# Prompt attention of a transformer block on one core: tiles unrolled, probabilities turned by transposes, the three branches scaled apart by factor rows that go through DRAM

## Chip, cores and metric

The kernel runs on one core of one Trainium2 chip. The metric is the device time of one execution in microseconds, the median of several runs.

## The reference

One layer of a decoder block on a prompt of 1024 tokens and on 8 sampled requests of 4 tokens: feed-forward, mixer, feed-forward, norm. Only the prompt's attention inside the mixer matters here. There are 8 query heads of width 64, in 2 groups that share keys and values. Each head has three branches: compressed attention over 64 block summaries, selected attention (with 1024 tokens and at most 16 blocks of 64 every causal key is selected) and a window of 512. Each branch has its own softmax and a gate for each token and head:

```python
s = jnp.einsum('btgrd,bngd->bgrtn', qg, kc).astype(jnp.float32) * ATTN_SCALE
p = masked_softmax(s, blk_end[None, :] <= q_pos[:, None])
...
o = gates[..., 0:1] * o_c + gates[..., 1:2] * o_s + gates[..., 2:3] * o_w
return jnp.concatenate([o.reshape(B, T, NSA_WIDTH), pool_out], axis=-1) @ w_out
```

## The kernel before, in words

The program is a sequence of stages with a barrier between them: compress the cache of the samples, feed-forward, input projection, pooling, compress the prompt, prompt attention (`stage_attend_prompt`, L1580), sample attention, output projection, feed-forward, finish. Each stage writes one program for each engine, and the engines meet by semaphores only; every engine works off its own list in order.

**Tiles.** The prompt attention has an outer loop (`Fori`) of two passes, one for each key head `g`, and in it eight tiles `qt` of 128 queries. Each tile has four steps `r`, one for each query head of the group. In a step the kernel makes the scores of head `r` of tile `qt` and at the same time a quarter of the value products of tile `qt-1`. After tile 7 a ninth round holds only value work (the drain), and the next pass then starts anew.

**Scores.** Keys and queries are doubled (POOL, `duplicate`, L1679), transposed on PE in turns of four (L1890) and split into a high and a low part by ScalarE (`high`, L1719) and VectorE (`low`, L1785). A pass begins with the `LEAD`, four turns for the keys and one for the first query tile. `selected_scores` (L1898) and `window_scores` (L1914, window and compressed keys together) write PSUM; VectorE takes the negated maxima (L1853, L1857, L1859), ScalarE the exponentials with their sums (L1757, L1763, L1765). They fill one PSUM tile each, so the next head's scores wait for the exponentials.

**Values.** A value unit is one block of up to 128 keys of one branch: tile `qt` has qt+1 selected units, min(qt+1, 5) window units and one compressed unit, 3, 5, 7, 9, 11, 12, 13 and 14 for tiles 0 to 7, 74 in a pass. In a unit PE multiplies the probabilities of the four heads by diagonal matrices (L1884), which transposes and scales them at once; ScalarE copies the high part (L1733), VectorE subtracts for the low part (L1798), and PE adds two products to one output bank (L1948, L1949). Turns alternate between two banks, so a turn waits for the subtraction of the turn two before. The product of a unit is issued behind the turn of the next. The order of turns is written out by `turns` and `steps` (L1618, L1622).

**Factors.** The diagonals hold gate divided by sum. VectorE makes the factors for two heads at a time after steps 2 and 3 (`factors`, L1802: three or four small operations), POOL multiplies them with an identity (L1700), and the first turn of the next tile waits for both (L1881).

**Output.** All three branches add up in one output bank, since they are already scaled. The upper half holds the product with the low part of the values; ScalarE copies it (L1738) and VectorE adds the halves for each head into `mixT` (L1830), one tile later.

SP has nothing to do in this stage. Queues of DMAs are idle in it but for instruction fetches.

```python
for h in range(GROUP):
    tr = pe.matmul(bank[0:rows, h * P:(h + 1) * P], probs[qt % 2][:, h, lo:lo + rows],
                   diag[:, qt % 2, h, branch, :], start=True, stop=True)
```

## Time and profile before

| | us |
|---|---|
| median of three runs | 3279.51 |
| lowest, highest | 3276.8, 3280.99 |
| the profiled execution | 3281.28 |
| its span | 3279.6 |
| PE busy | 2924.5 (89%) |
| VectorE busy | 1448.3 (44%) |
| ScalarE busy | 905.5 (28%) |
| POOL busy | 311.1 (9%) |

The stage of the change runs from about 1621 to 2099 us of the span. In the tables of windows and of groups PE is the multiplying part of TensorE and PEld its weight loads, DVE is VectorE, ACT ScalarE. A busy time is the time in which an instruction of the engine was under way; PEclk is the granted clock of TensorE as a share of 2.4 GHz, so 0.50 is 1.2 GHz. "idle before" of a group is the time its engine stood still directly before one of its instructions, with what ended it.

### The profile page before, as it was taken

What the parts mean: (1) busy time and instruction counts of PE and PEld (TensorE: products, weight loads), DVE (VectorE), ACT (ScalarE), POOL (GpSimd) and SP (SyncE); (2) the same over time, 40 slices, a digit from 0 to 9 for tenths busy, and PEclk for the clock granted to TensorE, in tenths of its full rate; (3) what the DMA queues carried; (4) which work ended last, traced back from release to release, by engine and by line L of the source; (5) the groups of instructions that cost most, each with busy time, mean ns of one, the idle gap of its engine ahead of it and who ended that gap; (6) DMA issues with size and microseconds to landing.
All of it is one profiled execution on the core that took longest, in us unless ns stands there. A gap on an engine that the chain in (4) does not pass through costs nothing. (4 is left out here: it accounts for less than half of the span.)

```text
span 3279.6 us, 48743 instructions
## 1 busy us (share of the span) xinstructions
PE 2924.5 (89%) x18374; PEld 2688.3 (82%) x18374; DVE 1448.3 (44%) x2808; ACT 905.5 (28%) x1537; POOL 311.1 (9%) x294
## 2 busy tenths in 40 slices
PE   4999989999999997885789789687799999999997
PEld 4889879999999996884667667433589999999996
DVE  4444455544444445013255456312326454444445
ACT  4665651111111102111245345233222111111112
POOL 3444410000000001000011011211000000000000
PEclk9999999999999998997579879888899999999999
DMA  4212133211111102102100000365322111111101
GB/s 158 110 56 110 62 105 105 64 38 38 40 50 42 47 0 87 33 26 77 35 1 1 2 1 1 125 183 158 112 58 62 42 53 49 38 38 51 38 13 53
DMA packets 168574, 193.84 MB, mean 59 GB/s; under 512 B 11431, under 2 KB 154536, under 8 KB 165679
## 3 DMA queue, kind: packets, MB, share of 16 engines
q1 hardware_dynamic: 161623, 141.58, 14.2%
q0 software_dynamic: 6816, 50.49, 4.2%
q8 instruction: 81, 1.33, 0.2%
q14 instruction: 54, 0.44, 0.0%
HBM read 178.30 MB, written 17.91 MB: 60 GB/s over the span
## 5 line engine op out<-in xcount | busy, mean ns | idle before, releaser
L407 ACT ACTIVATE f_act_gate<-f_act_gate 128x352 f32<-128x352 f32 x132 | 65.8, 498 | 1186.2 <-DVE f_act_gate L464 1186.1
L501 DVE SCALAR_TENSOR_TENSOR trunk<-f_down,trunk 128x352 f32<-128x352 f32 x528 | 275.8, 524 | 207.8 <-PE f_down L104 207.8
L102 PE MATMUL f_up<-f_h_hi,f_gu_hi 128*128 128x352 f32 x1056 | 344.6, 326 | 0.0
L102 PE MATMUL f_gate<-f_h_hi,f_gu_hi 128*128 128x352 f32 x1056 | 344.3, 326 | 0.0
L104 PE MATMUL f_up<-f_h_hi,f_gu_lo 128*128 128x352 f32 x1056 | 342.8, 325 | 0.0
L104 PE MATMUL f_gate<-f_h_hi,f_gu_lo 128*128 128x352 f32 x1056 | 342.5, 324 | 0.0
L102 PE MATMUL f_down<-f_a_hi,f_wd_hi 128*128 128x352 f32 x1056 | 340.6, 323 | 0.0
L103 PE MATMUL f_gate<-f_h_lo,f_gu_hi 128*128 128x352 f32 x1056 | 340.5, 322 | 0.0
L103 PE MATMUL f_up<-f_h_lo,f_gu_hi 128*128 128x352 f32 x1056 | 340.1, 322 | 0.0
L103 PE MATMUL f_down<-f_a_lo,f_wd_hi 128*128 128x352 f32 x1056 | 338.5, 321 | 0.0
L104 PE MATMUL f_down<-f_a_hi,f_wd_lo 128*128 128x352 f32 x1056 | 338.1, 320 | 0.0
L102 PE MATMUL cs_sum<-cs_x_hi,cs_w_hi 128*128 128x256 f32 (+1 forms) x768 | 229.9, 299 | 32.6 <-DVE cs_x_lo L1152 21.4
L104 PE MATMUL cs_sum<-cs_x_hi,cs_w_lo 128*128 128x256 f32 (+1 forms) x768 | 217.5, 283 | 0.0
L103 PE MATMUL cs_sum<-cs_x_lo,cs_w_hi 128*128 128x256 f32 (+1 forms) x768 | 217.4, 283 | 0.0
L102 PEld LDWEIGHTS f_gate<-f_h_hi,f_gu_hi 128*128 128x128 f32 x1056 | 199.6, 189 | 1.3 <-DVE f_gu_lo L447 1.1
L102 PEld LDWEIGHTS f_up<-f_h_hi,f_gu_hi 128*128 128x128 f32 x1056 | 199.9, 189 | 0.0
L1884 PE MATMUL at_turn_bank<-at_diag,at_probs 128*128 128x128 f32 (+1 forms) x1184 | 177.7, 298 | 24.6 <-POOL at_diag L1700 20.3
L1884 PEld LDWEIGHTS at_turn_bank<-at_diag,at_probs 128*128 128x128 f32 (+1 forms) x1184 | 162.4, 203 | 45.3 <-issue 39.6
L103 PEld LDWEIGHTS f_gate<-f_h_lo,f_gu_hi 128*128 128x128 f32 x1056 | 198.8, 188 | 0.2
L103 PEld LDWEIGHTS f_up<-f_h_lo,f_gu_hi 128*128 128x128 f32 x1056 | 198.9, 188 | 0.0
L103 PEld LDWEIGHTS f_down<-f_a_lo,f_wd_hi 128*128 128x128 f32 x1056 | 198.4, 188 | 0.0
L102 PEld LDWEIGHTS f_down<-f_a_hi,f_wd_hi 128*128 128x128 f32 x1056 | 198.1, 188 | 0.0
(333 smaller groups left out, 5812.3 us busy)
## 6 DMA issues: line engine op xcount, KB each, us to landing
as_pages<-in_cache_kv_slc_dram SPq DMA_DIRECT2D x192, 128.0 KB, 2.3
f_gu_raw<-in_w_ffn_gate_dram SPq DMA_DIRECT2D x44, 512.0 KB, 4.5
f_gu_raw<-in_w_ffn_up_dram SPq DMA_DIRECT2D x44, 512.0 KB, 5.7
f_wd_raw<-in_w_ffn_down_dram SPq DMA_DIRECT2D x22, 1024.0 KB, 5.0
as_pages<-in_cache_kv_slc_dram POOLq DMA_DIRECT2D x64, 128.0 KB, 3.2
in_w_raw<-in_w_in_dram SPq DMA_DIRECT2D x4, 1304.0 KB, 5.9
x_saved<-trunk SPq DMA_DIRECT2D x1, 4224.0 KB, 16.2
trunk<-x_saved SPq DMA_DIRECT2D x1, 4224.0 KB
```

The source lines that it names most:

```text
L102: pe.matmul(out, w_hi, x_hi, start=first, stop=False)
L103: pe.matmul(out, w_hi, x_lo, start=False, stop=False)
L104: return pe.matmul(out, w_lo, x_hi, start=False, stop=last)
L407: act.activation(act_gate[:, b, :], act_gate[:, b, :], ACT.Silu).then_inc(silu_done, 1)
L501: dve.scalar_tensor_tensor(xT[:, m, chunk(c)], down_bank[n % 4][:, 0:CH], 0.5, xT[:, m, chunk(c)], ALU.mult, ALU.add).then_inc(down_free, 1)
L1884: tr = pe.matmul(bank[0:rows, h * P:(h + 1) * P], probs[qt % 2][:, h, lo:lo + rows], diag[:, qt % 2, h, branch, :], start=True, stop=True)
```

## The change

The loop over two key heads becomes a straight list of 16 tiles `n`, with `g, qt = divmod(n, QT)`. The drain of tile 7 and the lead of tile 8 are interleaved, and only tile 15 has a drain by itself. All waits are on constants, and the no-ops before PE's groups are gone. In a step PE now issues the first turn, the window scores, the other turns, and then the selected scores of the next head.

Value turns are plain transposes of the exponentials. Each branch of a tile has an output bank of its own (two banks in turn). The factors of a tile, 12 columns in all (3 branches by 4 heads), are computed once by VectorE in the first step of the next tile, transposed on PE into 12 rows (a turn "f", first in step 1), copied by ScalarE, written to DRAM by SP (6 KB) and, when that has landed, read back by SP into all 128 partitions (`spread`, 768 KB). VectorE multiplies each branch's bank by its part of `spread` (`scale`), behind the first turn of the following branch; POOL adds the three branches and the two halves (`gather`). The key and value splits of the second head are made branch by branch, as the values of the first become free.

The core of the diff:

```diff
+            @block.sync
+            def _(sp):
+                for n in range(TILES):
+                    sp.wait_ge(hi_done, at[("f", n)] + 1)
+                    sp.dma_start(saved_rows[n % 2], factor_rows[:]).then_inc(rows_saved, 16)
+                    sp.wait_ge(rows_saved, 16 * (n + 1))
+                    if n:
+                        sp.wait_ge(scaled_done, 3 * n)
+                    sp.dma_start(spread[:].rearrange("p b r n -> p (b r) n"),
+                                 saved_rows[n % 2].unsqueeze(0).to_broadcast([P, ROWS, P])).then_inc(spread_landed, 16)
...
+                def gather(n):
+                    g, qt = divmod(n, QT)
+                    pool.wait_ge(scaled_done, 3 * n + 2)
+                    pool.tensor_tensor(scaled[:, 0], scaled[:, 0], scaled[:, 1], ALU.add).then_inc(added, 1)
+                    pool.wait_ge(scaled_done, 3 * n + 3)
+                    pool.wait_ge(added, 4 * n + 1)
+                    pool.tensor_tensor(scaled[:, 0], scaled[:, 0], scaled[:, 2], ALU.add).then_inc(added, 1)
+                    pool.wait_ge(added, 4 * n + 2)
+                    pool.tensor_copy(upper[:], scaled[HD:2 * HD, 0]).then_inc(added, 1)
+                    pool.wait_ge(added, 4 * n + 3)
+                    for half, sem in enumerate((added, out_taken)):
+                        pool.tensor_tensor(mixT[half * HD:(half + 1) * HD, 2 * g:2 * g + 2, qt * P:(qt + 1) * P],
+                                           scaled[0:HD, 0, half::2, :], upper[:, half::2, :], ALU.add).then_inc(sem, 1)
...
+    def lead(n):
+        own = [("k", n, b, half) for b in range(2) for half in range(2)] + [("q", n)]
+        values = quarter(n - 1, 0) if n else []
+        mixed = [x for pair in zip(own, values) for x in pair]
+        return mixed + own[len(values):]
+
+    def turns(n, r):
+        own = [("q", n + 1)] if r == 2 and n + 1 < TILES and not leads(n + 1) else []
+        if n == 0:
+            return own
+        values = [] if r == 0 and leads(n) else quarter(n - 1, r)
+        return ([("f", n - 1)] if r == 1 else []) + values + own
...
+                def scale(n, b):
+                    dve.wait_ge(pv_done, products[("v", n, ends[n][b])] + 1)
+                    dve.wait_ge(spread_landed, 16 * (n + 1))
+                    if n:
+                        dve.wait_ge(out_taken, n)
+                    dve.tensor_tensor(scaled[:, b], out_bank[(3 * n + b) % 2][:].rearrange("p (r n) -> p r n", r=GROUP),
+                                      spread[:, BRANCHES[b]], ALU.mult).then_inc(scaled_done, 1)
...
                     if x[0] == "v":
-                        _, qt, u = x
-                        branch, lo, rows, _ = value_units(qt)[u]
-                        if u == 0:
-                            pe.wait_ge(diag_ready, 2 * QT * g + 2 * (qt + 1) + ONE)
-                        pe.nop(nofuse=True)
+                        _, n, u = x
+                        branch, lo, rows, _ = value_units(n)[u]
+                        pe.wait_ge(exped[0 if branch == SLC else 1], GROUP * (n + 1))
                         for h in range(GROUP):
-                            tr = pe.matmul(bank[0:rows, h * P:(h + 1) * P], probs[qt % 2][:, h, lo:lo + rows],
-                                           diag[:, qt % 2, h, branch, :], start=True, stop=True)
+                            tr = pe.transpose(bank[0:rows, h * P:(h + 1) * P], probs[n % 2][:, h, lo:lo + rows],
+                                              K["ident"][:])
...
                     else:
-                        pe.wait_ge(dup_ready, DUPS * g + dups[x] + 1)
-                        pe.nop(nofuse=True)
-                        for i in range(4):
-                            tr = pe.transpose(bank[:, i * P:(i + 1) * P],
-                                              dup[dups[x] % 2][:, i].rearrange("p c d -> p (c d)"), K["ident"][:])
+                        pe.wait_ge(factor_ready, x[1] + 1)
+                        tr = pe.transpose(bank[0:ROWS, 0:P], factor[:, x[1] % 2].rearrange("p b r -> p (b r)"),
+                                          K["ident"][:])
...
+                for n in range(TILES + 1):
+                    for r in range(GROUP):
+                        xs = turns(n, r)
+                        first = lead(n) if r == 0 and leads(n) else xs[:1]
+                        rest = xs if r == 0 and leads(n) else xs[len(first):]
+                        for x in first:
+                            through(x)
+                        if r == 0 and leads(n):
+                            selected_scores(n, r)
+                        if n < TILES:
+                            window_scores(n, r)
+                        for x in rest:
+                            through(x)
+                        following = (n, r + 1) if r + 1 < GROUP else (n + 1, 0)
+                        if following[0] < TILES and not (following[1] == 0 and leads(following[0])):
+                            selected_scores(*following)
+                value_product()
...
+    saved_rows = nc.dram_tensor("saved_rows", [2, 12, P], F32).ap()
```

`through` issues a turn and then the product of the unit before it. VectorE's list follows PE's: the selected maximum, `low` of the first turn, the window maxima, the factors of the tile before (in step 0), `low` of the others with `scale` behind the unit that follows a branch's last one.

## Rows read from the trace of the kernel before

**Rows 1.** The page: its first line, PE's busy time, the granted clock in 40 slices.
```profile
span 3279.6 us, 48743 instructions
...
PE 2924.5 (89%) x18374; PEld 2688.3 (82%) x18374; DVE 1448.3 (44%) x2808; ACT 905.5 (28%) x1537; POOL 311.1 (9%) x294
...
PEclk9999999999999998997579879888899999999999
```

**Rows 2.** Windows of the stage: us, busy per engine, PEclk, DMA share, GB/s.
```profile
1621.00:1707.00 86.00, 66.59 (x333) 52.54 (x333) 42.98 (x112) 39.53 (x126) 15.56 (x16) 0.70 0.00 1
1707.00:1825.00 118.00, 106.88 (x679) 87.24 (x679) 69.98 (x135) 60.86 (x148) 13.41 (x11) 0.96 0.00 1
1825.00:1857.00 32.00, 26.03 (x147) 21.11 (x145) 11.91 (x22) 9.68 (x17) 2.63 (x3) 0.89 0.00 1
1857.00:1872.00 15.00, 4.89 (x20) 3.79 (x20) 4.60 (x9) 5.54 (x9) 2.45 (x4) 0.61 0.02 6
...
2067.00:2099.00 32.00, 23.73 (x142) 19.81 (x142) 12.87 (x26) 9.55 (x16) 1.47 (x1) 0.95 0.00 1
sum 478.00, PE 398.98 PEld 321.53 DVE 250.00 ACT 220.94 POOL 60.87; mean PE 57.00 PEld 45.93 DVE 35.72 ACT 31.56 POOL 8.70
```

**Rows 3.** Groups of instructions of the stage: busy, mean ns, idle before and its releaser.
```profile
L1884 PE MATMUL at_turn_bank<-at_diag,at_probs 128*128 128x128 f32 (+1 forms) x1184 | 177.7, 298 | 24.6 <-POOL at_diag L1700 20.3 <-PE at_out_bank L1949 2.1 <-DVE at_turned_lo L1798 1.0
...
L1798 DVE TENSOR_TENSOR at_turned_lo<-at_turn_bank,at_turned_hi 128x512 fp32r<-128x512 f32 (+1 forms) x148 | 102.1, 690 | 154.2 <-ACT at_turned_hi L1733 154.1
...
L1700 POOL TENSOR_TENSOR at_diag<-ident,at_factor 128x768 f32<-128x768 f32 x32 | 47.0, 1469 | 346.5 <-DVE at_factor L1821 346.5
...
L1830 DVE TENSOR_TENSOR trunk<-at_out_bank,at_upper 64x128 f32 x64 | 18.1, 283 | 15.0 <-ACT at_upper L1738 14.1
...
L1738 ACT ACTIVATE at_upper<-at_out_bank 64x512 f32<-64x512 f32 x16 | 9.5, 594 | 3.7 <-PEq L1953 3.4
...
L1815 DVE RECIPROCAL at_factor<-at_factor 128x6 f32<-128x6 f32 x32 | 6.1, 191 | 1.1
```

**Rows 4.** Timeline of PE in tile 6: start, length, instruction.
```profile
1780.63 0.64 PE L1890 MATMUL at_turn_bank<-ident,at_dup 128*128 128x128 f32 x4
1781.10 1.06 PE L1884 MATMUL at_turn_bank<-at_diag,at_probs 128*128 128x128 f32 x8
1781.91 0.47 PE L1948 MATMUL at_out_bank<-at_turned_hi,at_v_split 128*128 128x512 f32 x1
```

**Rows 5.** Timeline of PE: the first selected scores of tiles 1 and 4.
```profile
1643.76 0.33 PE L1910 MATMUL at_slc_bank<-diagonal,ident 128*128 128x128 bf16 x1
...
1706.69 0.23 PE L1910 MATMUL at_slc_bank<-diagonal,ident 128*128 128x128 bf16 x1
```

**Rows 6.** Timeline of PE: products in the drain of the first pass.
```profile
1849.59 0.47 PE L1948 MATMUL at_out_bank<-at_turned_hi,at_v_split 128*128 128x512 f32 x1 [0.22 <-DVE at_turned_lo L1798]
...
1852.76 0.47 PE L1948 MATMUL at_out_bank<-at_turned_hi,at_v_split 128*128 128x512 f32 x1 [0.22 <-DVE at_turned_lo L1798]
```

**Rows 7.** DMA issues: KB each, us from issue to landing.
```profile
op_w_raw<-in_w_out_dram SPq DMA_DIRECT2D x8, 512.0 KB, 4.1
...
f_wd_raw<-in_w_ffn_down_dram SPq DMA_DIRECT2D x22, 1024.0 KB, 5.0
...
cp_raw<-out_dram SPq DMA_DIRECT2D x1, 1024.0 KB, 13.7
...
cs_pe<-in_pe_cmp_k_dram SPq DMA_DIRECT2D x1, 8.0 KB, 1.7
...
gates_saved<-z SPq DMA_DIRECT2D x1, 3.0 KB, 4.0
```

**Rows 8.** Windows of the true transposes of L1236 and L2299 alone: busy, PEclk, DMA.
```profile
100.00:120.00 20.00, 4.22 (x28) 3.27 (x28) 1.00 0.62 224
...
2240.00:2260.00 20.00, 5.69 (x28) 4.39 (x28) 0.68 0.25 78
```

More of the change, by code:

```diff
@@ L1629, in stage_attend_prompt, with quarter @@
[L1629 to L1637 removed]
+    def quarter(n, r):
+        count = len(value_units(n))
+        return [("v", n, u) for u in range(count * r // GROUP, count * (r + 1) // GROUP)]
@@ new lines, in stage_attend_prompt @@
+    order = [x for n in range(TILES + 1) for r in range(GROUP)
+             for x in (lead(n) if r == 0 and leads(n) else []) + turns(n, r)]
+    at = {x: i for i, x in enumerate(order)}
+    dups = {x: i for i, x in enumerate([x for x in order if x[0] in "kq"])}
+    dup_order = list(dups)
+    values_order = [x for x in order if x[0] == "v"]
+    products = {x: i for i, x in enumerate(values_order)}
+    ends = [[max(u for u, unit in enumerate(value_units(n)) if unit[0] == branch) for branch in BRANCHES]
+            for n in range(TILES)]
@@ L1639, in stage_attend_prompt @@
+    behind = {}
+    for x, follower in zip(values_order, values_order[1:]):
+        if x[2] in ends[x[1]]:
+            behind[follower] = (x[1], ends[x[1]].index(x[2]))
     with ExitStack() as scope:
@@ L1950, in value_product @@
+                    pe.matmul(bank[:], values, turned_lo[v % RING][0:rows, :], start=False,
                               stop=last).then_inc(pv_done, 1)
[L1951 to L1973 removed]
@@ new lines, in through @@
+                def through(x):
+                    turn(x)
+                    value_product()
+                    if x[0] == "v":
+                        pending.append(x)
+                for n in range(TILES + 1):
+                    for r in range(GROUP):
+                        xs = turns(n, r)
+                        first = lead(n) if r == 0 and leads(n) else xs[:1]
+                        rest = xs if r == 0 and leads(n) else xs[len(first):]
+                        for x in first:
+                            through(x)
+                        if r == 0 and leads(n):
+                            selected_scores(n, r)
+                        if n < TILES:
+                            window_scores(n, r)
+                        for x in rest:
+                            through(x)
+                        following = (n, r + 1) if r + 1 < GROUP else (n + 1, 0)
+                        if following[0] < TILES and not (following[1] == 0 and leads(following[0])):
+                            selected_scores(*following)
```

465 lines of the change are left out of this document (226 added, 239 removed).

## The prediction, made before the changed kernel was run

> **What bounds the kernel now.** First the page: over the whole span PE is busy 89% of the time, and the granted clock is full in most slices but dips in those of the prompt attention, 19 to 25 [rows 1]. The change touches that stage alone, so the second view is the table of windows over it, from 1621 to 2099 us, 478 us of the span. Its seven stretches are two passes of one loop body over the two key heads: tiles 0 to 3 (86 us, PE busy 77%, mean clock 0.70), tiles 4 to 7 (118 us, PE busy 91%, clock 0.96), the drain of the last tile's 14 value units (32 us), and 15 us between the passes in which PE is busy 4.9 us [rows 2]. So three different limits: latency and a slow clock in the small tiles, PE in the large ones, and plain idleness at the seam. VectorE is busy 70 of the 118 us of the large tiles and ScalarE 61, so neither is far behind PE.
>
> Third, the groups of instructions with what they waited for [rows 3]. The 592 multiplications by a diagonal (L1884) are the stage's largest PE group: 1184 instructions, two for each product, while the true transposes of the doubled keys and queries are one each [rows 4]. PE stands idle 20.3 us before them waiting for the diagonals that POOL makes.
>
> Fourth, the timeline of PE at full clock in tile 6 [rows 4]. Four true transposes start at 1780.63 and what follows starts at 1781.10: 0.47 us. One turn through diagonals starts at 1781.10 and its successor at 1781.91: 0.81 us. A turn that is a true transpose is 0.34 us shorter.
>
> **The change, part by part** (negative is saved; all in us).
>
> a) *Turns become transposes.* 148 value turns, 0.34 each, 50 of PE time. What reaches the end depends on the limit. In the large tiles, where PE is the bound, there are 9+11+12+13 = 45 value units per pass, 90 in all: at most 90 x 0.34 = 31. In the drain, where the two-bank loop turn, copy, subtract, product binds, the products two units apart start at 1849.59 and 1852.76 [rows 6]: 3.17 for two, and shortening one turn per loop leaves 2.83, so 0.17 a unit. I take 0.27 for the 90: **-24** (0 to -31). The small tiles are latency bound: nothing.
>
> b) *No diagonals.* PE's 20.3 of waiting on POOL [rows 3] has no successor: the transposed operand is the exponentials, done before the tile ends. POOL's 47.0 of diagonals leaves with it. **-18** (-12 to -20).
>
> c) *The seam.* From 1825, when the first pass has its last scores, to 1872, when the second pass starts its first [rows 2], pass 47 us. In the new order the 14 value units of tile 7 lie between the five lead turns and the scores of tile 8. The same work on PE: 14 units at about 1.4 (1.59 less 0.17) is 20, the lead turns another 5, since their copies and subtractions alternate with those of values. 47 - 25 = **-22** (-10 to -32, the latter if tile 8's scores also run under the values).
>
> d) *The last drain and its end.* 14 x 0.17 = 2.4 saved; but after the last product come one scaling, then on POOL two adds of 128x512, a copy of 64x512 and two half adds. POOL's 128x768 multiply takes 1.47 [rows 3], so about 1.0 per full add and 0.6 for each of the rest: 4.5 in all with the scaling, against 0.59 + 4 x 0.28 = 1.7 for the copy and four adds now; the earlier branches are added while PE still works. **0** (-2 to +3).
>
> e) *VectorE.* Added: 48 scalings of 128x512 out of PSUM; the nearest row is the subtraction of the same shape, 0.690 [rows 3], so 33. Removed: 64 adds at 0.283, 18, and half of the factor operations, three of about 0.17 to 0.19 for 16 pairs, 8 [rows 3]. Net +7 on an engine that is busy 250 of the 478 us [rows 2]. **+4** (0 to +7). ScalarE loses 16 copies and gains 16 smaller ones: nothing. POOL trades 47 for about 16 x 4.3 = 69; it is busy 13% now, and its result is asked for more than a step later.
>
> f) *The turned factor rows.* 16 times a transpose on PE at 0.12, with a wait of PE for the factors, which VectorE now makes in the tile's next step; behind that wait stand the window scores. **+5** (+2 to +15).
>
> g) *The round trip through DRAM.* SP issues a 6 KB write and, when it has landed, a read of 768 KB into 128 partitions. No row shows a re-read of one place. The write: an 8 KB load lands in 1.7, a 3 KB store into DRAM in 4.0 [rows 7]; I take 2. The read: between 4.1 for 512 KB and 5.0 for 1024 KB of weights, 4.6; the highest row is 13.7, for 1024 KB read back from an output. With about 0.8 of issue and waits the trip is 7.4. The Trainium skill (DMA: Bandwidth & Descriptors, section on the anatomy of one DMA) gives 2.0 us and 436 GB/s, an estimate of 3.8 for the read; no run here shows it for a repeated source, and the sum would be some 10 lower by it. VectorE needs the rows at the first scaling, one step and about 1 us after the factor turn. A step in tiles 1 to 3 is (1706.69-1643.76)/12 = 5.2 now [rows 5], say 4.5 after; in tiles 4 to 7 (118/16) 7.4, say 6.5. So VectorE stands still about 2 in each of the four smallest tiles of a pass and hardly in the others, and behind it on its queue stand the window maxima, hence the exponentials, hence PE. 8 x 2 = **+16** (0 to +80).
>
> h) *Scores one step ahead.* The selected scores of the next head are issued before the step ends, and waits are on constants without extra no-ops. PE's waits for exponentials in the two kinds of scores and for issue are short and many. **-12** (0 to -20).
>
> i) *The clock.* Stretches with idle PE lose the full clock: 0.61 at the seam, 0.70 in the small tiles [rows 2]. A faster PE is idle more often in the large tiles; it may fall there at times, as at 1825 to 1857 (0.89). **+8** (0 to +40). A drain window at 0.95 and the large tiles at 0.96 speak against more. Stretches elsewhere with true transposes in the stream show both: full in one where they take 4.2 of 20 us, 0.68 in one where they take 5.7 [rows 8]. The Trainium skill (TensorE: Matmul & The Clock Gate, part 4, on transposes) says that the full clock doesn't engage for transposes; the first of these rows disagrees for a mixed stream, the second leaves room for it. That is a rival below.
>
> Sum: -24-18-22+0+4+5+16-12+8 = **-43**. The profiled execution took 3281.28 around a span of 3279.6; the median of the runs is 3279.51, so the sum is set against that: 3279.5 - 43 = **3237**.
>
> **The rivals.**
> 1. *The repeated read is slow, and VectorE waits for it in every tile: slower.* With R the whole trip and 6.5 the mean distance to the first scaling, the stall is 16 x (R - 6.5), against 59 saved by everything else. It decides at R = 10.2, a read of about 7.4. A read at 9.2, midway between 4.6 and 13.7, gives R = 12.0, +88 - 59 = +29: 3309. For: 6 KB read 128 times has no counterpart here. Against: the weight rows, and no other traffic in the stage (DMA share 0.00 in the windows). Chance 0.13.
> 2. *The clock falls in the large tiles.* PE's work there at full clock is 107 less 15 for the shorter turns, 92 per pass. With the clock at its lower level for half of the time that takes 92/0.75 = 123 instead of the 108 forecast, +30 for both passes: 3267; for the whole time 184, +152. The Trainium skill's sentence above points this way. For: the drop to 0.68 in rows 8. Against: PE gets busier as it slows, and the products and scores remain. Chance 0.12, a quarter of it slower than now.
> 3. *PE's saved time isn't used*: the chain turn, copy, subtract, product or VectorE binds in the large tiles too, and a) and h) are worth nothing: 3279.5 - 43 + 36 = 3272.5. For: VectorE and ScalarE at 60% and 52% there. Against: PE at 91%. Chance 0.12.
> 4. *PE's work sets the pace almost everywhere*, the trip is hidden and the seam disappears: -31-20-32-20+7 = -96 and with f) and i) 3195. Chance 0.13.
>
> Forecast case 0.50, from 3210 to 3262.
>
> **How the numbers follow.** The likeliest case gives 3237. The range has to take in rivals 2 to 4 and the foot of rival 1: 3190 to 3295, which leaves out about 0.2. About 0.2%, 6.6 us, is what a measurement of this kernel can tell from no change. Slower by more: rival 1 and a quarter of rival 2, 0.16. The same: a quarter of rival 2 and half of rival 3, 0.09. Faster: the rest, 0.75.
>
> **What would show it.** Right: one instruction for each turned head instead of two and 0.47 for a turn at full clock; no wait on POOL before turns; no stretch without scores or products at the middle of the stage; large tiles at about 27 us instead of 29.5; the spread landing about 4.6 after its issue; a VectorE wait for a DMA of 1 to 3 in small tiles only. Wrong: a spread that lands after more than 7 us, VectorE idle before scalings in all tiles, a granted clock under 0.85 in the large tiles, or a PE that is idle there on the subtractions by as much as its turns became shorter.

## The result and the profile of the changed kernel

The changed kernel takes **3173.5 us** (median of 4 runs, 3171.8 to 3174.5) beside 3280.3 for the kernel before (3276.8 to 3282.8). The ratio is 0.9675, with a 95% interval of 0.9658 to 0.9692: 107 us are saved where 43 were forecast, and the time lies below the range. The first lines of the page that answer to [rows 1], the changed kernel:

```profile
span 3172.3 us, 46324 instructions
...
PE 2825.5 (89%) x17798; PEld 2592.6 (82%) x17798; DVE 1457.5 (46%) x2742; ACT 904.5 (29%) x1536; POOL 338.6 (11%) x342
...
PEclk9999999999999999899559989789899999999999
```

PE does 99 us less and is still busy 89% of the span. The clock dips below 9 tenths in slices 19, 20, 23 and 25 (counted from 0), among others; the stage begins at 1620, in slice 20, so the 5 of slice 19 lies ahead of it, as most of slice 19 does before [rows 1]. Nearly all of the difference in time, 105 us, lies in the stage: it now lasts 373 us, from 1620, in place of 478. Its windows answer to [rows 2]; columns as there:

```profile
1620.00:1691.40 71.40, 56.09 (x275) 43.27 (x275) 43.06 (x99) 39.08 (x124) 14.88 (x20) 0.69 0.09 34
1691.40:1795.70 104.30, 87.22 (x551) 66.01 (x549) 80.33 (x131) 67.76 (x160) 26.20 (x31) 1.00 0.09 31
1795.70:1818.00 22.30, 19.53 (x107) 15.64 (x106) 12.24 (x28) 11.44 (x37) 2.22 (x4) 0.77 0.11 36
1818.00:1872.40 54.40, 44.64 (x218) 32.52 (x217) 36.00 (x78) 30.08 (x95) 15.97 (x18) 0.75 0.13 44
1872.40:1959.30 86.90, 74.74 (x475) 56.96 (x474) 68.84 (x114) 58.50 (x142) 19.69 (x22) 1.00 0.10 38
1959.30:1993.00 33.70, 20.96 (x122) 15.06 (x121) 18.62 (x29) 13.04 (x25) 9.16 (x10) 0.93 0.07 24
sum 373.00, PE 303.18 PEld 229.46 DVE 259.10 ACT 219.89 POOL 88.13; mean PE 50.53 PEld 38.24 DVE 43.18 ACT 36.65 POOL 14.69
```

The stretches are tiles 0 to 3 (71.4 us), tiles 4 to 7 (104.3), the seam up to tile 9 (22.3), tiles 9 to 11 (54.4), tiles 12 to 15 (86.9) and what follows the last selected scores (33.7). In the large tiles the clock is now 1.00, where it was 0.96 [rows 2]; the small tiles stand at 0.69 and 0.75, where tiles 0 to 3 stood at 0.70. The groups of instructions of the stage, changed kernel, answer to [rows 3]:

```profile
L1936 PE MATMUL at_turn_bank<-ident,at_probs 128*128 128x128 f32 (+1 forms) x592 | 97.4, 295 | 0.0
...
L2007 PE MATMUL at_out_bank<-at_turned_hi,at_v_split 128*128 128x512 f32 x132 | 68.3, 517 | 33.8 <-DVE at_turned_lo L1826 33.8
...
L1838 DVE TENSOR_TENSOR at_scaled<-at_out_bank,at_spread 128x512 f32<-128x512 f32 x48 | 32.6, 680 | 4.3 <-DMA at_spread<-saved_rows 4.0 <-PE at_out_bank L2008 0.2
...
L1869 DVE TENSOR_SCALAR at_factor<-at_sums 128x12 f32<-128x12 f32 x16 | 8.2, 512 | 0.1
...
L1878 DVE TENSOR_TENSOR at_factor<-at_factor,z 128x12 f32<-128x12 f32 x16 | 6.2, 386 | 0.6
...
L1945 PE MATMUL at_turn_bank<-ident,at_factor 128*12 128x128 f32 x16 | 4.9, 309 | 11.3 <-DVE at_factor L1878 11.3
```

L1936 is now one instruction a head: 97.4 us in place of 177.7 [rows 3]. No wait on POOL stands before it. PE's largest wait is for the subtractions (33.8), and VectorE waits 4.0 us for the spread in the whole stage. The factor turn (L1945), though, is waited for 11.3 us, and the two factor operations ahead of it take 512 and 386 ns on average. Before, on half as many columns, they took 162 and 166:

```profile
L1821 DVE TENSOR_TENSOR at_factor<-at_factor,z 128x6 f32<-128x6 f32 x32 | 5.3, 166 | 4.7 <-DVE at_factor L1818 0.5
L1813 DVE TENSOR_SCALAR at_factor<-at_sums 128x6 f32<-128x6 f32 x32 | 5.2, 162 | 4.5 <-ACT at_probs L1765 2.7 <-issue 1.8
```

Where the 107 went, by the length of the tiles (from the first diagonal block of selected scores of a tile to that of a later one, the points of [rows 5]):

| Stretch (us) | before | loop written out (experiment 1) | and transposes (4) | and no diagonals (4) | changed |
|---|---|---|---|---|---|
| tiles 1 to 3 | 62.9 | 62.0 | 55.0 | 49.7 | 50.9 |
| tiles 4 to 6 | 87.6 | 84.9 | 77.3 | 74.2 | 68.0 |
| start of tile 7 to start of tile 9 | 90.0 | 78.8 | 71.0 | 66.5 | 58.6 |
| tiles 9 to 11 | 64.5 | 61.4 | 55.1 | 49.8 | 54.4 |
| tiles 12 to 14 | 87.5 | 86.2 | 78.7 | 74.2 | 68.0 |

The three middle columns are experiments, told next; each column is one execution. Every stretch gives something: the two of small tiles 12.0 and 10.1 us, the two of large tiles 19.6 and 19.5, the seam 31.4. The transposes gave 7.0 and 6.3 in the small tiles, where the prediction had nothing. What came after the diagonals, from the fourth column to the last, gave 7.9 at the seam and 6.2 in each stretch of large tiles, but took 1.2 and 4.6 in the small ones.

### The profile page after: what moved, and what is told of

The parts are those of the page before. It is cut to its first block and busy times, and to the rows that moved or that the text cites. A ratio compares the mean times of both kernels' runs of the same rounds, so it can differ in the third digit from the quotient of the medians.

```text
span 3172.3 us, 46324 instructions
## 1 busy us (share of the span) xinstructions
PE 2825.5 (89%) x17798; PEld 2592.6 (82%) x17798; DVE 1457.5 (46%) x2742; ACT 904.5 (29%) x1536; POOL 338.6 (11%) x342
## 5 line engine op out<-in xcount | busy, mean ns | idle before, releaser
L102 PE MATMUL cs_sum<-cs_x_hi,cs_w_hi 128*128 128x256 f32 (+1 forms) x768 | 229.4, 299 | 33.8 <-DVE cs_x_lo L1152 22.6
L104 PEld LDWEIGHTS f_up<-f_h_hi,f_gu_lo 128*128 128x128 f32 x1056 | 198.0, 188 | 0.0
L104 PEld LDWEIGHTS f_gate<-f_h_hi,f_gu_lo 128*128 128x128 f32 x1056 | 198.0, 187 | 0.0
```

What stands on the lines that cost most here:

```text
L102: pe.matmul(out, w_hi, x_hi, start=first, stop=False)
L104: return pe.matmul(out, w_lo, x_hi, start=False, stop=last)
```

## The experiments

Times are medians; "saved" is against the kernel before as it ran beside them (medians of 3278.8 to 3282.8). Differences from the changed kernel are between sets of runs, and its interval of 0.0017 on either side of the ratio is 5.6 us: under that, one needs the trace. A trace is one execution, though. In four kernels whose large tiles have the same work in the same order (the changed one and those of experiments 8 and 9) tiles 4 to 6 take 68.0, 68.0, 68.0 and 68.9 us; tiles 1 to 3 take 50.9, 51.0, 47.6 and 48.0, at a granted clock of 0.77, 0.77, 0.86 and 0.86. So the large tiles can be compared to some tenths, but 3 us in a stretch of small tiles can be the clock alone.

**1. The loop alone.** The kernel before, its loop over the two key heads written out on four engines.

```diff
-                with pe.Fori(0, N_KV) as g:
+                for g in range(N_KV):
```

> The kernel before with its loop over the two key heads written out, so that every wait is on a constant and no register is worked out; order, diagonals, no-ops and the drain before the second lead stay. Theory 1 (the gain of 107 us comes from the merged seam, the shorter turns and the new order): only the jump at the seam (PE idle from 1856 to 1864 us) and a little at each wait go, 5 to 15 us faster than before, 3265 to 3275. Theory 2 (registers in front of each wait had slowed every handover between engines, and constants are most of the gain): 40 us or more faster, 3240 or less.

Measured: 3258.1, 0.9932 (0.9915 to 0.9948), 24 saved, between the two forecasts. This is the seam without any interleaving. Timeline of PE at the seam, the first lead turn of the second pass with the idle time before it, first in the kernel before, then in this one (start, length, instruction):

```profile
1864.02 1.86 PE L1890 MATMUL at_turn_bank<-ident,at_dup 128*128 128x128 f32 x8 [7.28 <-issue]
```

```profile
1849.01 1.06 PE L1890 MATMUL at_turn_bank<-ident,at_dup 128*128 128x128 f32 x8 [0.30 <-PE at_out_bank L1949]
```

Before, PE stood still 7.28 us between the last product of the first pass and the first lead turn, on issue: nothing in the records releases it but the loop's end. What takes the time there is not shown. Written out, the gap is 0.30. From tile 7 to tile 9 the loop is worth 11.2 us (table); the rest of the gain is spread over the tiles in pieces of 1 to 3 us, and some of it may be the clock.

**2. The transposes alone.** The kernel before, the loop kept and the diagonals still made and waited for. It leaves out the scaling by gate over sum.

```diff
-  tr = pe.matmul(bank[...], probs[...], diag[...], start=True, stop=True)
+  tr = pe.transpose(bank[...], probs[...], K["ident"][:])
```

> The kernel before with true transposes of the probabilities in place of the products with diagonals. The diagonals are still made and waited for, and leave the output: the value products are not scaled by gate over sum. Everything else stays. Theory 1: the shorter turns alone are worth 25 to 40 us in the old order (90 units of the large tiles at 0.3 to 0.46, little elsewhere): 3240 to 3255. Rival (the chain turn, copy, subtract, product binds in the old order, and only the new one can use shorter turns): under 15 us, 3265 or more.

Measured: 3235.3, 0.9867 (0.9850 to 0.9883), 47 saved, more than either forecast. The two groups of PE in the stage, this kernel:

```profile
L1884 PE MATMUL at_turn_bank<-ident,at_probs 128*128 128x128 f32 (+1 forms) x592 | 99.0, 294 | 27.1 <-POOL at_diag L1700 18.9 <-DVE at_q_split L1793 4.8 <-PE at_out_bank L1949 2.7
...
L1948 PE MATMUL at_out_bank<-at_turned_hi,at_v_split 128*128 128x512 f32 x132 | 65.4, 495 | 41.7 <-DVE at_turned_lo L1798 41.0
```

The turns take 78.7 us less than 177.7 [rows 3]. PE's wait for subtractions before the products is 41.7, so the loop of turn, copy and subtraction does bind in places (rival 3), but not enough to hold back the gain.

**3. The reverse: the changed kernel with products in place of transposes.**

```diff
-  tr = pe.transpose(bank[...], probs[...], K["ident"][:])
+  tr = pe.matmul(bank[...], probs[...], K["ident"][:], start=True, stop=True)
```

> The changed kernel with a real product with the identity (two instructions for each head) in place of each value transpose; nothing else differs. Theory 1 (PE sets the pace in the new order too, turns 0.46 us longer at 148 units): 40 to 60 us slower than the changed kernel, 3213 to 3233. Rival (PE has room in the new order, and VectorE or the chain sets the pace): under 20 us slower, 3193 or less.

Measured: 3216.6, 0.9807 (0.9791 to 0.9824), 43 above the changed kernel, as forecast for a PE that sets the pace. So the transposes are worth 43 to 47 from either side, and 40 (64 - 24) by experiment 4. Groups of PE, this kernel:

```profile
L1936 PE MATMUL at_turn_bank<-ident,at_probs 128*128 128x128 f32 (+1 forms) x1184 | 170.7, 292 | 0.0
...
L2007 PE MATMUL at_out_bank<-at_turned_hi,at_v_split 128*128 128x512 f32 x132 | 65.8, 499 | 15.2 <-DVE at_turned_lo L1826 14.5
```

The turns cost 73.3 us more of PE's time (170.7 less 97.4); the wait for the subtractions falls from 33.8 to 15.2 and gives 18.6 of it back. That leaves 54.7, against 43 measured. About 7 of the other 12 is PE's remaining work running faster: by the two pages PE is busy 66.5 us more (2892.0 less 2825.5) and not 73.3, and the small tiles have a clock of 0.86 where the changed kernel has 0.77. The rest lies in waits that these rows don't hold.

**4. Loop and transposes, then without the diagonals.** The second kernel also leaves out POOL's multiplications and the waits of PE and VectorE on them; its first turn waits for the exponentials. Both leave out the scaling by gate over sum.

```diff
-                        for pair in range(2):
-                            diagonals(g, qt, pair)
...
-                            pe.wait_ge(diag_ready, 2 * QT * g + 2 * (qt + 1) + ONE)
+                            for i in range(2):
+                                pe.wait_ge(exped[i], HEADS * g + GROUP * (qt + 1) + ONE)
```

> The kernel before with the loop written out and transposes in place of the products with diagonals, while the diagonals are still made and waited for (the output isn't scaled by them). It stands between two earlier runs and splits the 96 us of the one without diagonals. Theory (parts add): 22 to 24 + 45 = 67 to 69 faster than before, 3214 to 3216, so that the wait for POOL is worth some 28. Rival (parts overlap, the wait hides some of both): 3225 or more.

> The kernel before with the loop written out, transposes in place of the products with diagonals, and no diagonals made or waited for: the first turn of a tile waits for its exponentials. The output isn't scaled by gate over sum. Order, no-ops, drain, copy of the upper half and adds stay. Theory: 22 (loop written out) + 44 (transposes) + 15 to 20 (the wait for POOL, 18.9 us in the trace with transposes) = 81 to 86 faster than before, 3196 to 3201. Rival (the parts overlap, what one frees another takes): 3205 or more.

Measured: 3214.5, 0.9806 (0.9789 to 0.9822), 64 saved; and 3186.7, 0.9708 (0.9692 to 0.9725), 96 saved. The first is where it was forecast, so the loop and the transposes nearly add (24 + 47 = 71 against 64); the second saves 10 more than its forecast. The diagonals are worth 28 to 32 more. Of that the trace of the first shows about half, in PE's waits (us, times, longest; the releaser is not found there, but the wait goes with the diagonals):

```profile
PE at_turn_bank L1884 <- issue: 16.2, 14, 2.4
```

The rest stands in the windows of tiles 1 to 3, first with the diagonals, then without:

```profile
1639.80:1694.80 55.00, 43.61 (x211) 31.98 (x210) 31.81 (x81) 28.87 (x96) 10.55 (x10) 0.76 0.00 1
```

```profile
1641.80:1691.50 49.70, 37.95 (x212) 27.67 (x211) 31.60 (x81) 29.08 (x96) 1.84 (x3) 0.88 0.00 1
```

The small tiles lose 5.3 us, and PE's busy time there falls from 43.61 to 37.95 for the same instructions (211 and 212), since the granted clock is 0.88 in place of 0.76. PE over the whole span, from the two pages, again with the diagonals and without:

```profile
PE 2839.1 (88%) x17782; PEld 2598.4 (81%) x17782; DVE 1448.6 (45%) x2808; ACT 902.0 (28%) x1536; POOL 311.0 (10%) x294
```

```profile
PE 2822.4 (89%) x17782; PEld 2586.8 (81%) x17782; DVE 1449.0 (46%) x2808; ACT 902.3 (28%) x1536; POOL 264.8 (8%) x262
```

That is 16.7 less for the same 17782 instructions. So PE gained about as much in speed as in waiting. That the shorter waits are what kept the clock up is argued from these rows, not shown, and part of it may be the 3 us by which small tiles differ in any case. The gain in clock is not seen in the changed kernel, which has no diagonals either: its tiles 1 to 3 stand at 0.77.

**5. The DRAM trip lengthened.** SP reads the rows once or three times more before the read that counts.

```diff
+  for i in range(1):       # 3 in the second kernel
+      sp.dma_start(spread[...], saved_rows[...]).then_inc(extra_landed, 16)
+      sp.wait_ge(extra_landed, 16 * (n + i + 1))      # 3 * n + i + 1 in the second
   sp.dma_start(spread[...], saved_rows[...]).then_inc(spread_landed, 16)
```

> The changed kernel with the 768 KB read of every tile done twice, one after the other with a wait between, so that the rows are there about 4.3 us later. Theory (the trip has slack of some us in all but the small tiles): up to 12 tiles unaffected, the small ones 2 to 4 us each: 5 to 25 us slower, 3179 to 3199. Rival (the slack is gone already, each us counts in all 16 tiles): 16 x 4.3 = 69 slower, 3243.

> The changed kernel with the 768 KB read of every tile done four times in a row, so that the rows are there about 13 us later, as if one read took 17. Theory, with a slack of 2 us in the small tiles and 5 in the large ones: 16 x 13 - 8 x 2 - 8 x 5 = 150 us slower, 3325, beyond the kernel before. Rival (the two-bank output lets the products run ahead, and VectorE's wait costs less than its length): under 100 slower, 3273 or less.

Measured: 3222.2, 0.9824 (0.9801 to 0.9847), 49 more than the changed kernel; and 3359.1, 1.0245 (1.0228 to 1.0262), 186 more. Both are dearer than their theories had it; the first lies between its two forecasts, the second beyond both. VectorE's waits for the spread, twice and four times:

```profile
DVE at_scaled L1843 <- DMA at_spread<-saved_rows: 40.2, 12, 8.4
```

```profile
DVE at_scaled L1843 <- DMA at_spread<-saved_rows: 162.8, 16, 15.5
```

From one extra read to three, each adds (186 - 49)/2 = 68.5 us, 4.3 in each of 16 tiles. In the trace the three extra reads of tile 3 take 12.3 together, 4.1 each, so nearly all of that is delay times tiles; the clock fell as well. The first extra read cost 49 in place of 68.5, so about 20 us of it went into slack, 1.2 in a tile (the runs with it spread over 17 us, so this is good to about half); after that each us of delay costs about 16. Rival 1's mechanism exists. By this estimate it would have turned the change into a loss from (107 + 20)/16 = 7.9 us of delay on. The trip as it is, changed kernel, first the issue and the landing (ns; then us), then in tile 3 from the copy to the read's issue:

```profile
L1689 SPq DMA_DIRECT2D at_spread<-saved_rows x16: 319/320/333, 1646.5 to 1972.5; - x16
...
DMA to landing us min/median/max: 3.7/3.9/4.2
```

```profile
1675.64 0.27 ACT L1759 ACTIVATE at_factor_rows<-at_turn_bank 12x128 f32<-12x128 f32 x1 [0.77 <-PE at_turn_bank L1945]
...
1675.93 0.32 SPq L1685 DMA_DIRECT2D saved_rows<-at_factor_rows  x1
...
1677.21 0.32 SPq L1689 DMA_DIRECT2D at_spread<-saved_rows  x1
```

The read takes 3.9 (3.7 to 4.2), as the weights of 512 KB do with 4.1 [rows 7]: that one place is read 128 times shows no cost. The write lands within 1.28 of its issue. From the copy to the landing: 1677.21 + 3.9 - 1675.64 = 5.5, where 7.4 was taken. The Trainium skill (DMA: Bandwidth & Descriptors, section on the anatomy of one DMA) gave an estimate of 3.8 for the read. It fits its formula to transfers that GpSimd issues, and this one is issued by SP; the trace agrees even so.

**6. The factor turn, later and earlier.** It comes first in step 1, where PE waits 11.3 us for it. Later: behind the first value turn of the step. Earlier: VectorE makes the factors ahead of the window maxima of step 0 and not behind them.

```diff
-        return ([("f", n - 1)] if r == 1 else []) + values + own
+        if r == 1:
+            return values[:1] + [("f", n - 1)] + values[1:] + own
+        return values + own
```

```diff
                         turned_lo[...] ... ALU.subtract).then_inc(split, 1)
+                        if between:
+                            between()
                         if x in behind:
                             scale(*behind[x])
...
-                                low(x)
+                                low(x, early)      # factors(n - 1), in step 0
```

> The changed kernel with the turn of the factor rows moved behind the first value turn of step 1. PE stands idle 11.3 us before that turn, waiting for VectorE's factors, with the window scores behind it. Theory (that wait is on the path, and the trip through DRAM has slack): 5 to 15 us faster than the changed kernel, 3158 to 3168. Rival (the later rows make VectorE wait for the spread in the small tiles, where it already waits twice): the same or slower, 3172 or more.

> The changed kernel with VectorE's factors moved ahead of the third scaling and of the window maxima in step 0 (but in tile 8), so that POOL's second add does not run beside them. In the changed kernel the first factor operation lasts 0.51 us in the median and 0.17 at the least, and where it is long it ends within 0.05 us of the end of POOL's add. Theory 3 (a small VectorE operation is held up while POOL adds, and PE's 11.3 us of waiting before the factor turn are on the path): its median falls to under 0.25, PE's wait under 5 us, and the kernel is 5 to 15 us faster than the changed one, 3158 to 3168. Rival: the wait is covered, as the run with a later factor turn hints: within 4 us of 3173.5.

Measured, later: 3183.7, 0.9710 (0.9693 to 0.9726), 10 more than the changed kernel. The theory fell: the turn moved into the trip's slack. VectorE's wait for the spread there, in place of 4.0 (in an execution of 3194.5, where the other three took 3183.0 to 3183.8):

```profile
DVE at_scaled L1840 <- DMA at_spread<-saved_rows: 21.3, 10, 4.2
```

Measured, earlier: 3163.2 (3162.1 to 3166.9), 0.9641 (0.9625 to 0.9657), 10 less than the changed kernel, as forecast, and the fastest of all. The groups of this kernel:

```profile
L1950 PE MATMUL at_turn_bank<-ident,at_factor 128*12 128x128 f32 x16 | 4.9, 304 | 0.9 <-DVE at_factor L1880 0.7
...
L1871 DVE TENSOR_SCALAR at_factor<-at_sums 128x12 f32<-128x12 f32 x16 | 4.2, 260 | 0.2 <-ACT at_probs L1783 0.2
...
L1880 DVE TENSOR_TENSOR at_factor<-at_factor,z 128x12 f32<-128x12 f32 x16 | 3.1, 193 | 0.6
```

PE's wait is gone (0.9), and the two factor operations have shrunk to half without being changed. Why they were long: VectorE's timeline in the changed kernel, then POOL's over the same 3 us:

```profile
1715.46 0.50 DVE L1869 TENSOR_SCALAR at_factor<-at_sums 128x12 f32<-128x12 f32 x1
1716.00 0.23 DVE L1871 RECIPROCAL at_factor<-at_factor 128x12 f32<-128x12 f32 x1
1716.26 0.37 DVE L1878 TENSOR_TENSOR at_factor<-at_factor,z 128x12 f32<-128x12 f32 x1
```

```profile
1714.64 1.29 POOL L1714 TENSOR_TENSOR at_scaled<-at_scaled 128x512 f32<-128x512 f32 x1 [1.09 <-DVE at_scaled L1838]
1715.99 0.61 POOL L1716 COPY at_upper<-at_scaled 64x512 f32<-64x512 f32 x1
```

The factor operation L1869 starts while POOL adds the third branch to the sum of the others in SBUF, and ends at 1715.96, when the add does (1715.93). In 14 of 16 tiles it meets a POOL operation in that way, and its end is 0.03 to 0.04 behind POOL's end. L1878 takes 0.37 in 13 tiles; in the last, where it meets an add, it takes 0.99 and ends 0.04 behind the add. The reciprocal beside them takes 0.23 in all tiles. In the earlier place the same two operations of that tile take 0.17 and 0.18 us (from 1711.16 to 1711.81), with POOL's add from 1709.56 to 1710.83 out of the way. In 5 of the 16 tiles L1871 still meets an add, and takes 0.27 to 0.90. The Trainium skill (SBUF — State Buffer, section on who interferes with whom) says that VectorE and GpSimd share a pair of ports which one of them holds at a time, and that a VectorE instruction with two SBUF inputs contends with a GpSimd instruction that reads SBUF. The trace agrees, in that the last factor operation (two inputs in SBUF) is held up and the scaling, which has one (the other is in PSUM), is not (0.67 to 0.69 in the nine cases beside a POOL operation). L1869 has one SBUF input and is held up as well; in which mode it ran is not in the trace.

The edit moves the operations and shortens them at once, and the two were not told apart: 7.1 us (8.2 + 6.2 less 4.2 + 3.1) is what they became shorter by. Of the gain 8.7 us lies in the small tiles (50.9 to 46.3, and 54.4 to 50.2), where the clock rose from 0.77 and 0.75 to 0.90 and 0.86; the large tiles gained 1.5 in each stretch. So the 10 us are the edit's as a whole, and some of them may be the clock alone.

**7. The order of a step.** Two kernels: only PE puts its window scores ahead of the first turn; then PE, VectorE and ScalarE all go back to the old order, both scores and both maxima ahead of the first turn.

```diff
+                        alone = n < TILES and not (r == 0 and leads(n))
+                        if alone:
+                            window_scores(n, r)
                         for x in first:
...
                             through(x)
```

> The changed kernel with the window scores of a step moved ahead of its first turn on PE, so that they follow the selected scores directly as in the kernel before (the two leads stay as they are). The earlier run that was meant to test the order left the sequence on PE the same, since the end of one step and the start of the next are one place. Theory: a turn between the two kinds of scores feeds ScalarE and VectorE while the window's exponentials are finished, worth 10 to 30 us: 3184 to 3204. Rival: PE only trades one wait for another: within 6 us of 3173.5.

> The changed kernel with the order of the kernel before within a step on all three engines: both scores and both maxima ahead of the first turn, the window exponentials behind the second turn's copy. The run with PE's order alone put back was 61 us slower. Theory (it was slow because PE, ScalarE and VectorE then disagreed on the order, and the old order itself is as good): within 15 us of the changed kernel, 3166 to 3189. Rival (a turn between the two scores is worth much in any case): 40 us or more slower, 3214 or more.

Measured: 3234.3, 0.9855 (0.9839 to 0.9871), 61 more than the changed kernel and twice the upper end of its forecast; and 3196.0, 0.9736 (0.9720 to 0.9752), 22 more. The wait of PE before its window scores in the first (L1950, 31.2) and in the second (L1954, 7.8):

```profile
L1950 PE MATMUL at_win_bank<-at_kT_hi,at_q_split 128*128 128x512 f32 (+3 forms) x96 | 42.4, 442 | 31.2 <-ACT at_probs L1783 30.7 <-DVE at_kc_lo L1898 0.6
```

```profile
L1954 PE MATMUL at_win_bank<-at_kT_hi,at_q_split 128*128 128x512 f32 (+3 forms) x96 | 40.8, 424 | 7.8 <-ACT at_probs L1783 7.2 <-DVE at_kc_lo L1901 0.6
```

In the changed kernel it is 7.9. So the new order is worth 22 as a whole, between the two forecasts, and 39 of the 61 come from one engine's list standing across the others': PE waits for ScalarE to empty the window bank, and in VectorE's list the subtraction of the turn that PE now issues later still stands ahead of the window maxima. Most of the 22 is in the large tiles: tiles 4 to 6 take 74.8 with the old order on all three engines and 68.0 with the new, tiles 12 to 14 74.9 and 68.0, tiles 1 to 3 51.0 and 50.9. Over the stage PE waits 51 us for the subtractions before its products with the old order, in place of 36, and hardly any longer for the factors (0.5 in place of 11.3).

**8. The place of the selected scores, and the no-ops.** PE's selected scores at the start of a step, not at the end of the one before; and the no-ops back before PE's groups.

```diff
+                        if n < TILES and not (r == 0 and leads(n)):
+                            selected_scores(n, r)
...
+                        pe.nop(nofuse=True)
```

> The changed kernel with PE's order of scores put back: the selected scores of a head are issued at the start of its own step, ahead of the first turn, and not at the end of the step before. The orders of ScalarE and VectorE stay. Theory 1, in which the order hides the chain scores, maximum, exponential: 15 to 35 us slower than the changed kernel, 3189 to 3209. Rival, in which the order is worth no more than the 12 us forecast for it: 12 us slower or less.

> The changed kernel with a no-op put back ahead of each group of PE's instructions, so that the waits sit on it and not on the first weight load. Theory (a weight load behind a no-op starts later by about 0.05 us, some 450 groups, half of them on the path): 5 to 15 us slower, 3179 to 3189. Rival: hidden, within 3 us of 3173.5.

Measured: 3175.0, 0.9671 (0.9655 to 0.9687), and 3175.9, 0.9676 (0.9660 to 0.9692). The first is the same sequence on PE, since nothing stands between the end of one step and the start of the next; it tests nothing but how well two builds agree. The second is 2 us slower by the medians, which is too little to tell from nothing. Its trace can tell: tiles 4 to 6 and tiles 12 to 14 take 68.9 each, in place of 68.0. The end of a subtraction and the second product of the unit that waited for it, changed kernel, then with the no-ops:

```profile
1705.08 0.68 DVE L1826 TENSOR_TENSOR at_turned_lo<-at_turn_bank,at_turned_hi 128x512 fp32r<-128x512 f32 x1
1706.15 0.39 PE L2008 MATMUL at_out_bank<-at_turned_lo,at_v_split 128*128 128x512 f32 x1
```

```profile
1708.86 0.69 DVE L1826 TENSOR_TENSOR at_turned_lo<-at_turn_bank,at_turned_hi 128x512 fp32r<-128x512 f32 x1
1710.01 0.40 PE L2013 MATMUL at_out_bank<-at_turned_lo,at_v_split 128*128 128x512 f32 x1
```

That is 0.39 us from the end to the product (1705.76 to 1706.15) and 0.46 (1709.55 to 1710.01). Where PE stood idle for a subtraction, it is 0.38 to 0.41 in 42 of 45 cases without no-ops and 0.45 to 0.47 in 46 of 47 with them. So a no-op that carries a wait costs about 0.06 us each time PE is really waiting, near the 0.05 of the theory; PE stands idle 14 or 15 times in tiles 4 to 6, which makes the 0.9. There are fewer such waits than the theory had.

**9. The seam back.** The changed kernel, but with tile 7's 14 value units ahead of tile 8's lead, as before, and no loop.

```diff
-        mixed = [x for pair in zip(own, values) for x in pair]
-        return mixed + own[len(values):]
...
+        return [("f", n - 1)] + [x for r in range(GROUP) for x in quarter(n - 1, r)] + own
```

> The changed kernel with the seam put back: the factor turn and all 14 value units of tile 7 come before the lead of tile 8, whose scores run alone as in the kernel before. Everything else is kept, and there is no loop. Theory (the merged seam is worth what is left of the stretch from tile 7 to tile 9, 58.6 us now against 78.7 with the loop merely written out): 12 to 25 us slower than the changed kernel, 3186 to 3199. Rival (the gain at the seam is the loop's end alone): under 6 us.

Measured: 3180.7, 0.9691 (0.9674 to 0.9707), 7 more, or 5 by the ratios; the intervals overlap. By the traces the stretch from tile 7 to tile 9 takes 65.0 in place of 58.6, so the interleaving is worth about 6 there, not 12 to 25 as its theory had it: the loop's end had the larger part.

## Why the prediction was wrong

The direction was right, and so were most of its reasons for a gain; the size was not. The sum failed by 64 us. The terms that were too small, by 16 to 23 (a), 10 to 14 (b), 12 (g), 10 (h) and 7 to 9 (c), less 5 for f, make 50 to 63; i) had the wrong sign.

- **a) Turns become transposes (-24; measured -40 to -47).** This is the step that failed most, in two places. The price of a turn of true transposes, 0.47, was read from one that another turn follows [rows 4]. Followed by a value product, as value turns are, a turn of four is 0.35 in the changed kernel (1981.53 to 1981.88):

```profile
1981.53 0.60 PE L1936 MATMUL at_turn_bank<-ident,at_probs 128*128 128x128 f32 x4
1981.88 0.48 PE L2007 MATMUL at_out_bank<-at_turned_hi,at_v_split 128*128 128x512 f32 x1
```

  The kernel of experiment 2 shows both prices one behind the other, 0.47 (1981.51 to 1981.98) and 0.35 (1981.98 to 1982.33). So the 0.12 goes with what follows, and not with the diagonals; why is not shown:

```profile
1981.51 0.63 PE L1890 MATMUL at_turn_bank<-ident,at_dup 128*128 128x128 f32 x4
1981.98 0.60 PE L1884 MATMUL at_turn_bank<-ident,at_probs 128*128 128x128 f32 x4
1982.33 0.48 PE L1948 MATMUL at_out_bank<-at_turned_hi,at_v_split 128*128 128x512 f32 x1
```

  So 0.46 is saved a turn at full clock (0.81 less 0.35), and over the stage 80.3 (177.7 less 97.4) where 50 was worked out. And "the small tiles are latency bound: nothing" was wrong: tiles 1 to 3 lost 7.0 us by the transposes alone (62.0 to 55.0), tiles 4 to 6 7.6. At the lower clock a turn goes from about 1.7 to about 0.7. That it stands in the chain of every step there is argued, not shown. A large tile takes 22.7 us (68.0/3) where about 27 was forecast; it took 29.2 before, and the transposes alone account for 2.5 of the difference.
- **b) No diagonals (-18; measured -28 to -32).** The recorded waiting of 20.3 was taken as an upper bound. In the old order PE also ran faster afterwards, by 16.7 of busy time, a gain that the changed kernel's small tiles don't show.
- **c) The seam (-22; measured -24 for the loop, and -5 to -7 for the interleaving).** The size was right for the 15 idle us, but the cause was not named: PE's 7.3 at the loop's end were taken for lead turns and splits. Half of the loop's 24 lies outside the seam, and the stretch from tile 7 to tile 9 as a whole lost 31.4, with the transposes and the diagonals.
- **d) The drain and its end (0).** The end costs what was forecast: from the end of the last product to that of the last add the changed kernel needs 4.9 (1986.84 to 1991.71), the kernel before 2.0, so +2.9, where 4.5 - 1.7 = 2.8 was worked out. The drain saved more than the 2.4 taken: tile 15 with its scores and its drain went from 61.9 to 51.3, and 7.2 of that came with the transposes (60.5 to 53.3). The timeline of the end, changed kernel:

```profile
1986.45 0.39 PE L2008 MATMUL at_out_bank<-at_turned_lo,at_vc_split 64*128 64x512 f32 x1
1986.79 1.26 POOL L1711 TENSOR_TENSOR at_scaled<-at_scaled 128x512 f32<-128x512 f32 x1 [15.14 <-DVE at_scaled L1838]
...
1990.20 1.51 POOL L1719 TENSOR_TENSOR trunk<-at_scaled,at_upper 64x256 f32<-64x256 f32 x2
```

  The last row is two half adds. POOL's adds of 128x512 take 1.26 here, where about 1.0 was taken.
- **e) Scalings (+4).** 0.680 each against 0.690 taken, and VectorE is busy 9 more in the stage (259.1 less 250.0), where 7 was worked out: the size was right; what of it reached the end was not tried.
- **f) The factor turn (+5; measured about +10).** Within its bounds, by the wait of 11.3 and by what experiment 6 gained. That POOL's adds would lengthen the factor operations was not foreseen.
- **g) The trip (+16; measured about +4).** The trip was 5.5 in place of 7.4, and it waited in two tiles, not in eight. The step lengths (4.5, 6.5) were about right. The lower estimate for the read, 3.8 in place of 4.6, would have taken 8 x 0.8 = 6 off this term and not "some 10".
- **h) Scores one step ahead (-12).** No such change of sequence exists: the end of one step is the start of the next. What PE's list gained is a turn between the two kinds of scores, and this is worth 22. The term also held the waits on constants and the no-ops; the part of the loop's 24 that lies outside the seam and about 0.06 us for each wait of PE belong here.
- **i) The clock (+8).** Wrong in sign: the large tiles went from 0.96 to 1.00. The Trainium skill (TensorE: Matmul & The Clock Gate, part 4, on transposes) says that the full clock doesn't engage for transposes. The window of tiles 4 to 7 at 1.00 disagrees for a mixed stream: of its 551 PE instructions 192 are transposes of probabilities (L1936).

Of the rivals, the fourth (PE sets the pace almost everywhere, 3195) came nearest, and was too small by 22; its own terms add up to 3196.5. Rival 3's chain can be seen (33.8 us of waits for the subtractions), but takes back less than a third of what the transposes save (18.6 of 73.3 in experiment 3). Rival 1 would have needed 7.9 us more in the trip; rival 2 had no part.

The measured parts, 64 for the loop and the transposes, 28 to 32 for the diagonals, 5 to 7 for the interleaving and 22 for the order, less 10 for the factor turn and 4 for the trip, come to 105 to 111, against 107. That it closes so well is partly luck: the parts were taken at either end of the change, part of the diagonals' gain doesn't show in the changed kernel's small tiles, and what the scalings take was not tried by itself.

## What to carry to other kernels

Price a short operation from a place where it is followed by what will follow it, and price it at the lower clock as well: the small tiles, taken to be bound by latency and worth nothing, gave as much by the transposes as the large ones. Where a table of lists gives the order of work on several engines, change all of them together or none; one list out of step cost 39 us here, more than the order itself was worth. A result that goes through DRAM and comes back one step later is cheap as long as the slack is known: find it by making the trip longer, and move the work in front of it, not behind.

## What the runs showed of the hardware

- Small VectorE operations in SBUF (128x12) were held until POOL's add or copy had ended: 0.17 became 0.40 to 0.86, and 0.18 became 0.37 to 0.99; the reciprocal (0.23), and scalings and subtractions that read PSUM (0.67 to 0.69), were not lengthened.
- A read of 6 KB into 128 partitions, 768 KB in all, landed in 3.7 to 4.2 us.
- The end of a loop on four engines kept PE idle for 7.3 us.
- A wait of PE that sat on a no-op cost it 0.06 us more than one on its own instructions (0.45 to 0.47 and 0.38 to 0.41 from the end of a subtraction to the second product).
- Four transposes of 128x128 took 0.35 us of PE ahead of a product and 0.47 ahead of another turn, at full clock.
- Without the waits for diagonals the granted clock in tiles 1 to 3 was 0.88 in place of 0.76, for the same instructions of PE; between kernels that are alike there it was 0.77 or 0.86, and 50.9 or 47.6 us.
